# Depthwise convolution on TensorE: tap matrices loaded from memory in place of matrices that VectorE writes

## The reference

```python
def conformer_conv_module(h, w_pw1, b_pw1, w_dw, b_dw, ln_g, ln_b, w_pw2, b_pw2):
    a = h @ w_pw1 + b_pw1
    u = a[..., :CONV_CH] * jax.nn.sigmoid(a[..., CONV_CH:])
    y = lax.conv_general_dilated(
        u, w_dw[:, None, :].astype(u.dtype), window_strides=(1,),
        padding=[(CONV_WIDTH - 1, 0)],
        dimension_numbers=('NWC', 'WIO', 'NWC'),
        feature_group_count=CONV_CH) + b_dw
    y = jax.nn.silu(layer_norm(y, ln_g, ln_b))
    return y @ w_pw2 + b_pw2
```

## Time and profile before

| | us |
|---|---|
| median of 3 runs | 1875.03 |
| lowest, highest | 1874.86, 1875.82 |
| the profiled execution | 1876.46 |
| its span from first to last instruction | 1874.5 |

### The profile page before, as it was taken

How to read it: one execution, slowest core, us unless ns; L and a number is a source line. 1 busy time by engine, 2 the same in 40 slices (tenths; PEclk the granted TensorE clock), 3 DMA queues, 4 the chain that set the end, 5 groups by cost and what they waited for, 6 DMA issues and landing times.

```text
span 1874.5 us, 24976 instructions
## 1 busy us (share of the span) xinstructions
PE 1854.0 (99%) x9297; PEld 1557.3 (83%) x9297; DVE 1024.0 (55%) x1470; ACT 645.4 (34%) x965; POOL 28.0 (1%) x54
## 2 busy tenths in 40 slices
PE   8999999999999999999999999999999999999998
PEld 6888888887698888888988888889898888888886
DVE  5534434688767434435764343458766784344345
ACT  5322322445744222223532222235213553122223
POOL 0000000031000000000000000000000000000000
PEclk9999999999999999999999999999999999999999
DMA  5333233422023233233233332232443323333231
GB/s 191 113 101 101 90 101 99 126 75 64 12 91 101 92 99 101 90 94 108 80 120 93 92 101 99 90 112 83 129 127 93 90 79 93 102 98 101 91 100 57
DMA packets 62103, 181.59 MB, mean 97 GB/s; under 512 B 7088, under 2 KB 16448, under 8 KB 62032
## 3 DMA queue, kind: packets, MB, share of 16 engines
q1 hardware_dynamic: 60432, 179.09, 30.5%
q0 software_dynamic: 1600, 1.51, 0.3%
HBM read 173.63 MB, written 6.29 MB: 96 GB/s over the span
## 4 chain that ended last, share of the span: by engine, by line
PE 95%; DVE 2%; DMA 1%; ACT 1%; issue 1%; POOL 0%; SPq 0%; DVEq 0%; ACTq 0%
PE bank L365 27%; PE bank L366 27%; PE bank L367 27%; PE bank L431 4%; PE bank L747 3%; PE bank L436 2%; PE bank L382 1%; PE bank L679 1%; PE bank L695 1%; PE bank L405 1%; PE bank L660 1%; PE bank L406 1%; PE bank L409 1%; PE bank L389 1%; DMA w_raw<-stream 0%
## 5 line engine op out<-in xcount | busy, mean ns | idle before, releaser
L1101 DVE TENSOR_TENSOR w_lo<-w_raw,w_hi 128x1024 fp32r<-128x1024 f32 x302 | 369.3, 1225 | 430.4 <-ACT w_hi L842 419.6
L365 PE MATMUL bank<-x_hi,w_hi 128*128 128x512 f32 x1432 | 558.8, 390 | 0.0
L367 PE MATMUL bank<-x_hi,w_lo 128*128 128x512 f32 x1432 | 557.2, 389 | 0.0
L366 PE MATMUL bank<-x_lo,w_hi 128*128 128x512 f32 x1432 | 557.1, 389 | 0.0
L842 ACT ACTIVATE w_hi<-w_raw 128x1024 fp32r<-128x1024 f32 x302 | 317.1, 1055 | 598.8 <-PE bank L367 586.7
L365 PE MATMUL bank<-a_hi,w_hi 128*128 128x512 f32 (+1 forms) x882 | 329.0, 373 | 0.0
L366 PE MATMUL bank<-a_lo,w_hi 128*128 128x512 f32 (+1 forms) x882 | 327.5, 371 | 0.0
L367 PE MATMUL bank<-a_hi,w_lo 128*128 128x512 f32 (+1 forms) x882 | 327.4, 371 | 0.0
L367 PEld LDWEIGHTS bank<-x_hi,w_lo 128*128 128x128 f32 x1432 | 268.8, 188 | 55.9
L365 PEld LDWEIGHTS bank<-x_hi,w_hi 128*128 128x128 f32 x1432 | 268.9, 188 | 55.3
L366 PEld LDWEIGHTS bank<-x_lo,w_hi 128*128 128x128 f32 x1432 | 268.9, 188 | 55.2
(11 more groups left out here) (187 smaller groups left out, 1436.8 us busy)
## 6 DMA issues: line engine op xcount, KB each, us to landing
w_raw<-stream SPq DMA_DIRECT2D x312, 512.0 KB, 3.5
h_resid<-xT SPq DMA_DIRECT2D x8, 256.0 KB, 7.2
w_raw<-stream SPq DMA_DIRECT2D x8, 256.0 KB, 6.8
u_scratch<-V SPq DMA_DIRECT2D x8, 256.0 KB, 2.1
a_lo<-u_scratch SPq DMA_DIRECT2D x8, 256.0 KB, 2.8
qT<-z_scratch SPq DMA_DIRECT2D x8, 256.0 KB, 3.5
outT<-h_resid SPq DMA_DIRECT2D x8, 256.0 KB, 2.2
z_scratch<-kT SPq DMA_DIRECT2D x4, 256.0 KB, 2.3
```

What stands on the lines that cost most here:

```text
L365: nc.tensor.matmul(out, lw[0], lx[0], start=first, stop=False)
L366: nc.tensor.matmul(out, lw[0], lx[1], start=False, stop=False)
L367: return nc.tensor.matmul(out, lw[1], lx[0], start=False, stop=last)
L1101: nc.vector.tensor_tensor(w_lo[:, s, :], raw[:, s, :], w_hi[:, s, :].bitcast(F32), ALU.subtract).then_inc(s_lo, 1)
```

## The change

The 32 tap matrices now lie ready in memory, zeros included, each 128 x 1152 float32 (576 KB, or 0.590 MB; 18.9 MB in all). SP loads them into five buffers in turn: three in `f_out`, `tap_matrix` and a new `tap_matrix2`. Matrix k goes to buffer k mod 5 once group k-5 is convolved. The first five are loaded at j = 0, once the mean square of the stage's input has been turned into a root (before, `f_out` is in use). VectorE's `matrices` is gone, and the loads of the bare taps (0.6 MB in all) with it. The matmuls and their order are unchanged, but each group waits for its buffer's load.

```diff
-            def load_taps(j):
-                if j >= 2:
-                    sp.wait_ge(s_mat, GROUPS * (j - 1))
-                sp.dma_start(taps[:, j % 2, :, :, :].rearrange("p g m q -> p (g m q)"), taps_in[j, :, :]
-                             ).then_inc(s_taps[j % 2], 16)
+            def load_matrices(j):
+                for k in range(MATS + GROUPS * (j - 1) if j else 0, min(MATS + GROUPS * j, GROUPS * KD)):
+                    if j:
+                        sp.wait_ge(s_cv, k - MATS + 1)
+                    sp.dma_start(mats[k % MATS], mats_in[k // GROUPS, k % GROUPS, :, :]).then_inc(s_mats[k % MATS], 16)
...
-            load_taps(0)
-            load_taps(1)
             for j in range(KD):
                 n = PW1 + 2 * RING + 2 * j
                 load(n, n % RING)
+                if 3 <= j < KD - 1:
+                    load_matrices(j - 2)
+                if j == KD - 1:
+                    load_matrices(6)
                 if j == KD - 1:
                     load_y(4)
                     store_z(5)
                 load(n + 1, (n + 1) % RING)
-                if 2 <= j < KD - 1:
-                    load_taps(j)
+                if j == 0:
+                    sp.wait_ge(s_root, 3 * 4 + 1)
+                    load_matrices(0)
+                if j == KD - 2:
+                    load_matrices(5)
                 store_u(j)
...
                 load_groups(j)
+                if j == KD - 1:
+                    load_matrices(7)
                 if j == KD - 2:
                     for i in range(4):
                         load_y(i)
-                    load_taps(KD - 1)
                     store_z(4)
...
                     for g in groups:
-                        pe.wait_ge(s_mat, GROUPS * j + g + 1)
+                        k = GROUPS * j + g
+                        pe.wait_ge(s_mats[k % MATS], 16 * (k // MATS + 1))
...
-                def matrices(j):
-
-                    shape = [P, SHIFTS, GC, PH]
-                    dve.wait_ge(s_taps[j % 2], 16 * (j // 2 + 1))
-                    for g in range(GROUPS):
-                        if j:
-                            dve.wait_ge(s_cv, GROUPS * (j - 1) + g + 1)
-                        nc.vector.tensor_tensor(mats[g], same_c[:, None, :, None].broadcast_to(shape),
-                                                taps[:, j % 2, g, :, None, :].broadcast_to(shape), ALU.mult
-                                                ).then_inc(s_mat, 1)
```

More of the change, by code:

```diff
@@ L138, in build_program @@
         ug = al[:, 0:2 * GROUPS * (PAD + NT)].rearrange("p (i g n) -> p i g n", i=2, g=GROUPS)
-        taps = sb("taps", [P, 2, GROUPS, SHIFTS, PH])
-        conv_c = sb("conv_consts", [P, GC + P + KD * GROUPS])
-        same_c, same_q, b_dw = conv_c[:, 0:GC], conv_c[:, GC:GC + P], conv_c[:, GC + P:]
+        conv_c = sb("conv_consts", [P, P + KD * GROUPS])
+        same_q, b_dw = conv_c[:, 0:P], conv_c[:, P:]
         extra = sb("tap_matrix", [P, SHIFTS * P])
@@ L145, in build_program @@
         swapped = [*(a_lo[:, k, :].bitcast(F32) for k in range(KD)), spare[:, 0:T], spare[:, T:2 * T]]
-        flat = (fv[:, i * SHIFTS * P:(i + 1) * SHIFTS * P] for i in range(KD * T // (SHIFTS * P)))
-        mats = [m.rearrange("p (m c q) -> p m c q", m=SHIFTS, c=GC) for m in (*flat, extra[:, :])]
+        MAT = SHIFTS * P
+        extra2 = sb("tap_matrix2", [P, MAT])
+        mats = [*(fv[:, i * MAT:(i + 1) * MAT] for i in range(3)), extra[:, :], extra2[:, :]]
+        MATS = len(mats)
         kf = kT[:, :, :].rearrange("p a n -> p (a n)")
@@ L206, in build_program @@
         s_sig, s_u = sem("gate_sigmoid"), sem("u_ready")
-        s_taps = [sem(f"taps_loaded{i}") for i in range(2)]
+        s_mats = [sem(f"tap_matrix_loaded{i}") for i in range(MATS)]
         s_ud = [sem(f"u_in_dram{i}") for i in range(2)]
@@ L212, in build_program @@
         s_bm = sem("bias_less_mean")
-        s_mat, s_cv, s_zg = sem("tap_matrix_ready"), sem("group_convolved"), sem("z_groups_ready")
+        s_cv, s_zg = sem("group_convolved"), sem("z_groups_ready")
         s_early = sem("early_groups_added")
@@ L1424, in conv @@
                         if (j, e) == (KD - 1, 0):
-                            matrices(6)
                             bias_less_mean(5)
@@ L1428, in conv @@
                     gate(j)
-                    if 1 <= j < KD - 2:
-                        matrices(j - 1)
                     if 2 <= j < KD - 2:
@@ L1442, in conv @@
                             centre(i)
-                        matrices(5)
                         bias_less_mean(4)
                         centred(4)
-                matrices(7)
                 add_squares(1)
@@ L1560, in tables, with tap_matrices @@
     return rc, rs, np.eye(P, dtype=np.float32), mask
-def tap_places(w):
-    out = np.zeros((KD, GC, PH, GROUPS, SHIFTS, PH), w.dtype)
+def tap_matrices(w):
+    out = np.zeros((KD, GROUPS, GC, PH, SHIFTS, GC, PH), w.dtype)
+    c = np.arange(GC)
     w = w.reshape(CW, KD, GROUPS, GC)
@@ L1571, in tap_places @@
                 if 0 <= tap < CW:
-                    out[:, :, p, :, m, q] = w[tap].transpose(0, 2, 1)
-    return out.reshape(KD, P, GROUPS * TAPS)
+                    out[:, :, c, p, m, c, q] = w[tap]
+    return out.reshape(KD, GROUPS, P, SHIFTS * P)
 def group_tables():
     i = np.arange(P)
-    same_c = (i[:, None] // PH == np.arange(GC)[None, :]).astype(np.float32)
-    same_q = (i[:, None] % PH == i[None, :] % PH).astype(np.float32)
-    return same_c, same_q
+    return (i[:, None] % PH == i[None, :] % PH).astype(np.float32)
 def kernel(x, norm_pre, norm_post, w_ffn_in, w_ffn_out, attn_w_qkv, attn_b_qkv, attn_w_o, attn_b_o, attn_sinks,
@@ L1614 @@
     rc, rs, ident, mask = tables()
-    same_c, same_q = group_tables()
+    same_q = group_tables()
     b_groups = np.broadcast_to(b_dw.reshape(KD * GROUPS, GC, 1), (KD * GROUPS, GC, PH)).reshape(KD * GROUPS, P).T
@@ L1619 @@
            "rope_c": rc, "rope_s": rs, "ident_in": ident, "ident_b_in": ident.astype(bf),
-           "mask_in": mask.astype(bf), "taps_in": tap_places(w_dw.reshape(CW, D)),
-           "conv_in": np.concatenate([same_c, same_q, b_groups], 1)}
+           "mask_in": mask.astype(bf), "mats_in": tap_matrices(w_dw.reshape(CW, D)),
+           "conv_in": np.concatenate([same_q, b_groups], 1)}
     nc = bacc.Bacc("TRN2", target_bir_lowering=False, num_devices=1, dynamic_dma_scratch_size=4096)
```

4 lines of the change are left out of this document (2 added, 2 removed).

## The result

| | before | changed |
|---|---|---|
| median, us (22 runs each) | 1875.18 | 1878.24 |
| lowest, highest | 1874.12, 1876.42 | 1876.20, 1880.15 |
| the profiled execution, its span | 1876.46, 1874.5 | 1878.08, 1876.1 |

The ratio is 1.0016, with a 95% interval of 1.001 to 1.0021: 3.06 us more by the medians, so slower, and clear of the noise, but inside the 0.2% (3.75 us) that the prediction counted as no change. 1878.0 had been predicted. The changed kernel's runs also scatter more, over 4.0 us against 2.3.

What follows compares the result with a forecast made beforehand. TensorE, busy 99%, was taken as the bound, with late DMA loads the cost. Convolve 0, chunks 1 to 3 and convolve 4 at 0, convolve 7 at 2.8 and thin covers at 0.2 gave +3.0 us: 1878.0, range 1874.5 to 1884.0.

Steps and rivals of the forecast that it cites:

- What bounds the kernel, and VectorE's 43 us at nothing: Whole kernel: TensorE is busy 99%, no wait of it names VectorE's 32 writes, so removing their 43 us gains nothing.
- Rival C: End of the convolution stage: less VectorE work shortens it by 1.6 us, to 1873.4; chance 0.03.
- Convolve 0, hidden by 0.3 us: Stage's start: u(0) and ug(0) queue behind matrices 0 to 4, ug(0) landing at 1322.1, 0.3 us to spare.
- convolve 0 is late by over 1 us: Start of convolve 0: a delay beyond this was named beforehand as a sign that the prediction is wrong.
- Chunks 1 to 3 and convolve 4, nothing: Middle of the stage: each matrix has a round's time in chunks 1 to 3; convolve 4's is hidden by 0.3 us.
- Convolve 7, +2.8 us: Stage's last chunk: the never-empty queue delays u(7)'s store, so ug(7) lands at 1433.5 and TensorE waits 2.8 us more.
- Rival A: Convolution stage: the queue keeps up at 371 to 406 GB/s, costing 0 to +1 us, 1875.0 to 1876.0; chance 0.24.
- B's 304 GB/s: Rival of a queue too slow in the stage: at 304 GB/s +9.2 us, 1884.2; chance 0.37 for over +3.75.
- Inside convolve 7: Matrices 29 to 31 stand behind ug(7); the first lands near 1435.1, needed at 1435.5.
- all thin covers together: Convolve 0 and convolve 4: 0.2 us added for their covers of 0.3 us.
- the signs named beforehand: Profile after: VectorE some 981 us, ug(7) wait 2 to 4 us, matrix waits under 0.5, DMA share 1390 to 1431 over 0.95.

Runs made afterwards that it cites:

- The kernel without the writes: Kernel before without VectorE's 32 writes of tap matrices, TensorE multiplying what lies in the buffers; 1874.52 us, ratio 0.9999.
- w23 late: Changed kernel with the loads of w23 and y(5) moved behind matrices 29 to 31; 1876.24 us, ratio 1.0008.
- matrix 29 in w23's place: Changed kernel with matrix 29 loaded where w23 was, ahead of u(7), and w23 and y(5) behind matrices 30 and 31; 1877.38 us, ratio 1.0009.
- changed, again: The changed kernel measured once more, no edit, beside the kernel before; 1876.68 us, ratio 1.0013.
- matrices held: Changed kernel with matrices 29 to 31 issued only once ug(7) has landed; 1878.8 us, ratio 1.0019.
- the split start: Changed kernel with only matrices 0 and 1 loaded ahead of u(0)'s store, 2 to 4 behind the load of ug(0); 1876.11 us, ratio 1.0008.
- the short matrices: Changed kernel loading only 512 of each matrix's 1152 columns (0.262 MB instead of 0.590), same order and waits; 1874.4 us, ratio 1.0.
- the best variants: Changed kernel with the split start, with w23 and y(5) loaded last, or with both; 1876.11, 1876.24 and 1875.81 us.

## Why the prediction was right in sum, and where its terms were off

**What bounds the kernel, and VectorE's 43 us at nothing: right.** The kernel without the writes gains 0.1 us by the medians and nothing in the stage's length, and TensorE still waits 0.85 us for the last bias. Rival C is out.

**Convolve 0, hidden by 0.3 us: wrong, and this is the largest error.** It costs 1.22 and 1.28 us in the two profiles of the changed kernel. The prediction's own limit, "convolve 0 is late by over 1 us", is passed. The failed step is the landing of u(0): the sum had it 5.0 us after its issue, and it took 6.51 and 6.60. Matrices in a row moved faster than the 360 GB/s taken (394 and 399), but two things were missed. The queue was slow to start (250 GB/s from 1308 to 1310) and fell to 336 and 340 with the store in the mix, so that the five rows from 1308 to 1318 come to 344 on the mean. And the sum put only 0.4 us between the last bytes and the landing. In the last microsecond before u(0) landed the DMA share was 0.09 in the changed kernel (33 GB/s), and 0.04 to 0.17 in the other four profiles with this start: the landing comes well behind the bulk of the bytes. In the kernel before, with nothing else on the queue, that share was 0.51. Over the five profiles with this start the loss follows that one time:

| kernel | u(0) issued to ug(0) issued | loss ahead of convolve 0 |
|---|---|---|
| w23 late | 5.77 | 0.38 |
| matrix 29 in w23's place | 5.91 | 0.71 |
| changed | 6.51 | 1.22 |
| changed, again | 6.60 | 1.28 |
| matrices held | 6.97 | 1.63 |

In each row the first number less the second is 5.2 to 5.4: that is what can be hidden, and the prediction's 5.0 + 0.3 was the same. The cover was right, the transfer was not. The store's time differs by 1.2 us between executions of the same code at this point, which fits the wider scatter of the runs.

**Chunks 1 to 3 and convolve 4, nothing: right for the changed kernel,** but with less spare than "a round's time". With the split start a delay of 1.3 to 1.6 us on SP was enough to make matrix 5 late. The step read the need of each matrix and not the place of its issue, behind a load that waits for a store.

**Convolve 7, +2.8 us: the mechanism was right, the size was not.** TensorE waits for ug(7), as said, but the entry costs 0.66 us (0.85 in the repetition). The term that failed is the landing of u(7): the sum had it 4.9 us after its issue, and it took 2.55 and 2.79. The sum gave the 12.85 MB up to and with u(7) 38.9 us, which is 330 GB/s, from 360 for large rows and 273 for small transfers; with a full queue they moved at 356 from 1391 to 1426, and large rows alone at up to 422. So the backlog was nearly through when u(7) was issued, where the prediction had over 4 us of it left. What still costs is w23 behind the end of that backlog: with w23 moved away, 2.02 us and a wait of 0.27. Rival A (the queue keeps up, 0 to 1 us) describes this place better than the forecast did, and B's 304 GB/s is far off.

**Inside convolve 7** a matrix was 0.39 us late in one of two profiles. The prediction had 0.4 us of cover here, and 0.2 for all thin covers together.

**Sum.** 0 + 2.8 + 0.2 was predicted. The profiles give 1.2, 0.7 to 0.9, and 0 to 0.65, with 0.2 and 0.4 us spread over the rest: 2.5 and 2.7 us for the stage (137.86 and 138.11 against 135.37). The medians say 3.06 and, in the repetition, 2.06. So the total of +3 was met because one term was 1.2 too small and another 2 too large. The sign, and that the loss is two late small transfers behind matrices, were reasoned; that the number was within 0.3 us was luck, since two errors of opposite sign cancelled. Of the signs named beforehand, VectorE's 983 us and the matrices' wait under 0.5 us came true. The wait for ug(7), 0.82 us, was not 2 to 4, and the DMA share from 1390 to 1431, 0.93, was not over 0.95.

The rate itself can be set beside a page. The Trainium skill, "DMA: Bandwidth & Descriptors", section "Bandwidth", has 341 GB/s for a transfer of 1 MB and 425 for one of 16 MB, on a lone core and issued from GpSimd. Here transfers of 0.59 MB, issued from SP with the next ones already queued, reach 422: in this trace a row of loads goes by the figure of the long transfer, and not by that of its own size. The same section says that a share of about 358 GB/s binds transfers between HBM and SBUF; the 422 measured here on a lone core is above it.

**Left open:** why ug(7) takes 3.49 us with the short matrices, why the landing of u(0) differs by 1.2 us between executions, and how much of the last 1.1 us of the best variants is real, since their intervals hold none.

## What to carry to other kernels

Moving work from an engine that nobody waits for to a queue that somebody waits in gained nothing here and lost 2 to 3 us: look first for the waits that name the engine, and if none does, for the smallest urgent transfer on the queue. Price that transfer by the bytes that haven't moved yet when it is issued, whenever they were issued, and read the DMA share just ahead of it: the same slot ahead of u(7) cost nothing on a queue with room and 0.2 to 0.8 us on a full one. Put only as many loads ahead of it as are needed first. When a delay is cured by moving loads behind, follow them to the next transfer that waits in the same order, since their bytes are still in front of somebody.

## What the runs showed of the hardware that I had not expected

- Loads of 0.590 MB in rows of 4.6 KB, queued one behind another, moved at up to 422 GB/s over 2 us, more than any stretch of the kernel before that I had read (406).
- A store of 0.262 MB that lands in 2.0 us in a free queue took 5.8 to 7.0 us behind five loads of 0.590 MB, and 2.4 to 2.7 us behind two. Between executions of the same order it differed by up to 1.2 us.
- A slot of 0.524 MB issued 2.6 us ahead of such a store cost it 0.2 to 0.8 us (2.22 to 2.83 us against 2.02) where the slot lay behind a backlog, at a DMA share of 0.89 to 0.99 ahead of the store, and nothing (2.01 to 2.05) at 0.70 to 0.79.
- A store behind a full queue landed well after most engines had nothing left to move: in the last 1 us before u(0) landed the DMA share was 0.04 to 0.17, in five profiles.
